# Seven products in place of eight for two K-tile pairs in ten of eleven feed-forward up strips

## The reference

```python
def swiglu(x, w_up, w_down):              # w_up (2048, 2*5632), w_down (5632, 2048)
    g, u = jnp.split(x @ w_up, 2, axis=-1)
    return (jax.nn.silu(g) * u) @ w_down

h = h + 0.5 * rms_norm(swiglu(rms_norm(h, ffn1_pre), ffn1_up, ffn1_down), ffn1_post)
h = h + rms_norm(hybrid_mixer(...), mix_post)
h = h + 0.5 * rms_norm(swiglu(rms_norm(h, ffn2_pre), ffn2_up, ffn2_down), ffn2_post)
```

## Time and profile before

| | us |
|---|---|
| median of 3 runs | 2435.23 |
| lowest and highest | 2434.61, 2436.49 |
| span of the profiled execution, first to last instruction | 2433.9 |
| PE busy in it | 2415.4 (99%) |
| DVE busy | 1289.5 (53%) |
| ACT busy | 1149.2 (47%) |

### The profile page before, as it was taken

The page is one execution under the profiler, slowest core; times in us unless marked ns, Lnnn a source line. Parts: engine busy times, 40 slices in busy tenths (PEclk is TensorE's granted clock), DMA queues, the critical chain, the costliest instruction groups (busy, mean ns, idle before and its releaser), DMA issues.

```text
span 2433.9 us, 32932 instructions
## 1 busy us (share of the span) xinstructions
PE 2415.4 (99%) x10823; PEld 1985.5 (82%) x10823; DVE 1289.5 (53%) x1395; ACT 1149.2 (47%) x1340; POOL 41.6 (2%) x48
## 2 busy tenths in 40 slices
PE   9999999999999999999999999999999999999998
PEld 7888888888887788887888888888888888888887
DVE  5455554544447555555545555555555555554444
ACT  6454544533435454454544444444554454544443
POOL 1000000000001000000000000000000000000000
PEclk9999999999999999999999999999999999999999
DMA  8566665766565555565656666655566665665664
GB/s 256 187 217 193 211 215 182 225 199 195 192 189 183 156 170 177 164 186 159 199 183 202 192 192 195 192 182 178 176 216 216 190 218 184 219 209 196 190 196 158
DMA packets 271357, 470.91 MB, mean 193 GB/s; under 512 B 21056, under 2 KB 65776, under 8 KB 270928
## 3 DMA queue, kind: packets, MB, share of 16 engines
q1 hardware_dynamic: 269648, 464.60, 61.2%
q0 software_dynamic: 1488, 5.68, 0.8%
q10 hardware_dynamic: 176, 0.07, 0.0%
HBM read 456.64 MB, written 2.10 MB: 188 GB/s over the span
## 4 chain that ended last, share of the span: by engine, by line
PE 94%; SPq 2%; DVE 2%; DMA 1%; ACT 1%; issue 1%; DVEq 0%; ACTq 0%; POOL 0%; POOLq 0%
PE acc L580 31%; PE acc L582 30%; PE acc L581 30%; SPq L424 2%; PE bank L601 1%; DMA w_raw<-in_ffn_up_dram 1%; DVE w_lo L1221 1%; ACT w_hi L923 0%; DMA w_raw<-in_ffn_down_dram 0%; PE bank L824 0%; PE bank L764 0%; PE bank L790 0%; DVE xT_lo L1232 0%; DVE hid_sb L1359 0%; PE bank L845 0%
## 5 line engine op out<-in xcount | busy, mean ns | idle before, releaser
L1221 DVE TENSOR_TENSOR w_lo<-w_raw,w_hi 128x1024 fp32r<-128x1024 f32 x856 | 1045.0, 1227 | 1062.1 <-ACT w_hi L923 1052.5
L923 ACT ACTIVATE w_hi<-w_raw 128x1024 fp32r<-128x1024 f32 x856 | 902.5, 1060 | 1192.7 <-PE acc L582 1040.3
L580 PE MATMUL acc<-w_hi,xT_hi 128*128 128x512 f32 x2464 | 968.8, 393 | 6.1 <-DVE xT_lo L1232 3.9
L582 PE MATMUL acc<-w_hi,xT_lo 128*128 128x512 f32 x2464 | 960.1, 390 | 0.0
L581 PE MATMUL acc<-w_lo,xT_hi 128*128 128x512 f32 x2464 | 959.6, 389 | 0.0
L580 PEld LDWEIGHTS acc<-w_hi,xT_hi 128*128 128x128 f32 x2464 | 463.0, 188 | 110.0 <-DVE w_lo L1221 7.6
L582 PEld LDWEIGHTS acc<-w_hi,xT_lo 128*128 128x128 f32 x2464 | 462.9, 188 | 97.0
L581 PEld LDWEIGHTS acc<-w_lo,xT_hi 128*128 128x128 f32 x2464 | 463.2, 188 | 95.2 <-issue 1.0
L580 PE MATMUL acc<-w_hi,act_hi 128*128 128x512 f32 x704 | 274.2, 389 | 1.5 <-DVE w_lo L1221 1.5
L581 PE MATMUL acc<-w_lo,act_hi 128*128 128x512 f32 x704 | 273.9, 389 | 0.0
L582 PE MATMUL acc<-w_hi,act_lo 128*128 128x512 f32 x704 | 273.9, 389 | 0.0
(11 more groups left out here) (144 smaller groups left out, 911.7 us busy)
## 6 DMA issues: line engine op xcount, KB each, us to landing
w_raw<-in_ffn_up_dram SPq DMA_DIRECT2D x352, 512.0 KB, 4.4
w_raw<-in_ffn_down_dram SPq DMA_DIRECT2D x176, 512.0 KB, 4.7
w_raw<-in_w_gate_dram SPq DMA_DIRECT2D x96, 512.0 KB, 4.1
w_raw<-in_w_in_dram SPq DMA_DIRECT2D x72, 512.0 KB, 3.7
w_raw<-in_w_in_dram SPq DMA_DIRECT2D x128, 256.0 KB, 3.0
w_raw<-in_w_ret_out_dram SPq DMA_DIRECT2D x32, 512.0 KB, 4.6
w_raw<-in_w_out_dram SPq DMA_DIRECT2D x32, 512.0 KB, 4.5
hid_T<-blocks SPq DMA_DIRECT2D x352, 32.0 KB, 1.8
```

Source lines behind the costliest of these rows:

```text
L580: pe.matmul(pair[m][:, :], xh, wh, start=(first and kk == 0), stop=False)
L582: mm = pe.matmul(pair[m][:, :], xl, wh, start=False, stop=(last and kk == KG - 1))
L923: act.activation(w_hi[:, s, :], w_raw[:, s, :], ACT.Copy).then_inc(w_rounded, 1)
L1221: dve.tensor_tensor(w_lo[:, s, :], w_raw[:, s, :], w_hi[:, s, :].bitcast(f32), ALU.subtract).then_inc(w_split, 1)
```

## The change

Strip 1 of each feed-forward block stays as it was (section `first{f}`). In the other ten, two of the eight K-tile pairs (K-tile pairs 6 and 7 of 0 to 7) are computed by Strassen's scheme over the 2x2 blocks token tile by K tile and K tile by gate/up. For such a pair PE makes 7 products of 3 passes (21 instructions) in place of 8 (24).

- DVE makes the four weight sums `t_raw` from the gate group and the up group of the pair (`sum13`, one operation of 1024 columns; `sum24`, two chained of 512). ACT rounds them, DVE takes their rests (two operations of 1024 columns each). In the up group only the second K tile is still split (512 columns).
- The four input sums `s_raw` are made once per block, during strip 1; PE transposes four scaled tiles for them, and waits for `s_split` ahead of the loop.
- PE's order in a strip: groups 0 to 3, pair by Strassen (groups 4 and 5), 6, 7, 8, 9, pair by Strassen (10 and 11), 12 to 15. Gate is complete at group 11.
- Products 1, 5, 6 and 7 go to four PSUM banks. DVE combines them: at step 11 and 12 the gate (`u2`, `u3`, `u4`, `u5`, `gate_sb`), at the end of the strip up (`hid_sb`, L1664 and L1666 of the changed kernel), then the product with the silu'd gate (L1671), then the block transposes. ACT's silu moves from step 7 to step 13.
- The turned activations go to `act_raw`, a place for each strip. Their split moves out of the up strips: the first two at steps 14 and 15 of the last up strip, the others at every second step of the first turn of down. PE's group `n` of down waits for the split of strip `n // 2`.
- `u2` to `u5` lie where `post_gain` is, so POOL loads `post_gain` only when the last up strip has been read. DVE waits for it ahead of the loop of down.

```diff
+QUADS = ((4, 5, 6), (10, 11, 7))
-                        sp.dma_start(hid_T[to * SQ:(to + 1) * SQ, q, :, :, :],
+                        sp.dma_start(act_raw[to * SQ:(to + 1) * SQ, ds(p, 1), q, :, :, :].rearrange("p a m k i -> p (a m) k i"),
                                      blocks[q * SQ:(q + 1) * SQ, to, :, :, :]).then_inc(hid_landed, 16)
...
+                with sp.Fori(0, NST) as i:
                     for n in range(2 * GD):
                         if n == 2 * SLOTS:
-                            with sp.If(i > 0):
-                                turn_hidden(f, before(i, NUP))
+                            turn_hidden(f, i)
+                        if n - SLOTS in QUAD_GATE:
+                            sp.wait_ge(t_summed, 3 * (quad(f, i, QUAD_GATE[n - SLOTS]) + 1))
+                            sp.sem_inc(slot_summed, 1)
...
+            rsqrt("pre2", rs_pre[:, 2, :])
+            wait_strip_read(pool, "up1", NST - 1, 1)
             pool.dma_start(post_gain[:, :], on_all(t["ffn2_post"][0], D)).then_inc(gain_landed, 16)
...
+            def seven_products(f, i, j):
...
+                pe.wait_ge(w_split, group(sec, i, ng) + 1 + SLOTS)
+                p1 = three(bank[0][:, :], *x(0), *w(ng, 0), first, last)
...
+                three(gate[0][:, :], *x(1), *w(ng, 1), False, last).then_inc(w_used, 1)
...
+                pe.wait_ge(w_split, group(sec, i, nu) + 1 + SLOTS)
+                three(upper[0][:, :], *s(3), *w(nu, 1), first, False).then_inc(w_used, 1)
+                pe.wait_ge(t_split, 2 * quad(f, i, j) + 1)
+                p7 = three(bank[3][:, :], *s(2), *tt(1), first, last)
+                p5 = three(bank[1][:, :], *s(0), *tt(0), first, last)
+                pe.wait_ge(t_split, 2 * quad(f, i, j) + 2)
+                p6 = three(bank[2][:, :], *s(1), *tt(2), first, last)
...
+                three(gate[1][:, :], *a22, *tt(3), False, last).then_inc(t_used, 1)
...
+                with dve.Fori(0, NST) as i:
                     for n in range(2 * GD):
+                        if n + SLOTS in QUAD_GATE:
+                            sum13(f, i, QUAD_GATE[n + SLOTS])
                         rest_group(sec, i, n)
+                        if n + SLOTS in QUAD_GATE:
+                            sum24(f, i, QUAD_GATE[n + SLOTS])
+                        if n in T_AT:
+                            j, pair = T_AT[n]
...
+                            dve.tensor_tensor(t_pair(t_lo, j, pair), t_pair(t_raw, j, pair),
+                                              t_pair(t_hi, j, pair).bitcast(f32), ALU.subtract).then_inc(t_split, 1)
...
+                    dve.wait_ge(silu_done, NST * f + i + 1)
+                    wait_strip_read(dve, sec, i, 1)
                     for m in range(MT):
+                        last = dve.scalar_tensor_tensor(hid_sb[:, m, :], hid_sb[:, m, :], rs_pre[:, 2 * f, m:m + 1],
+                                                        gate_sb[:, m, :], ALU.mult, ALU.mult)
+                    last.then_inc(combined, 1)
+                    wait_combined(dve, f, i, "hid")
+                    turn_blocks()
```

More of the change, by code:

```diff
@@ L91, in bank_uses, with strassen @@
     use("gains", 3)
+    def strassen(f):
+        use(f"s{f}", 2, 3)
+        for _ in range(NST):
+            use(f"p{f}", 0, 1, 2, 3)
     transposed("x0")
+    strassen(0)
     transposed("x1")
@@ L668, in tail, with three @@
                 tile_by_tile(product, range(total - SLOTS, total), {(1, SLOTS - 2): pieces})
-            def swiglu(f):
[L671 to L678, removed]
-                        head(product, i, lambda c, m: transpose_h(2, c, m))
-                    for n in range(SLOTS if f == 1 else 0, 2 * GD):
-                        product(n)
-                        if f == 0 and n in (0, 2, 4):
-                            with pe.If(i < 1):
-                                for half in range(2):
-                                    transpose_x(n // 2 + 1, half)
+            def three(dst, xh, xl, wh, wl, start, stop):
+                pe.matmul(dst, xh, wh, start=start, stop=False)
+                pe.matmul(dst, xh, wl, start=False, stop=False)
+                return pe.matmul(dst, xl, wh, start=False, stop=stop)
@@ L922, in round_it @@
                     act.wait_ge(w_used, group(sec, i, ahead) + 1)
-                    act.activation(w_hi[:, s, :], w_raw[:, s, :], ACT.Copy).then_inc(w_rounded, 1)
+                    cols = w_cols(sec, ahead)
+                    act.activation(w_hi[:, s, cols], w_raw[:, s, cols], ACT.Copy).then_inc(w_rounded, 1)
                 if sec == "kv" and ahead >= GD:
@@ L989, in hidden_hi @@
                 for m in range(MT):
-                    last = act.activation(act_tile(act_hi, p, m), hid_tile(m), ACT.Copy)
+                    last = act.activation(act_tile(act_hi, p, m), raw_tile(p, m), ACT.Copy)
                 last.then_inc(hid_rounded, 1)
@@ L1005, in output_strips @@
                     round_group(sec, i, n)
[L1006 to L1007 removed]
+                    if hook is not None:
+                        hook(n)
                 def tile0():
@@ L1028, in swiglu @@
             def swiglu(f):
+                sec = f"first{f}"
+                for n in range(2 * GD):
+                    round_group(sec, 0, n)
+                    if f == 0 and n in (0, 2):
+                        x_hi(n // 2 + 2)
+                    if n == (3 if f == 0 else 2):
+                        if f == 0:
+                            for c in range(CH):
+                                act.wait_ge(x_landed[c], 16)
+                        input_squares(2 * f)
+                    if n == GD - 1:
+                        wait_strip(act, sec, 0, n)
+                        act.wait_ge(rs_ready, MEAN[f"pre{2 * f}"] + 1)
+                        pair = pair_of(sec, 0)
+                        for m in range(MT):
+                            last = act.activation(gate_sb[:, m, :], acc[pair][m][:, :], ACT.Silu,
+                                                  scale=rs_pre[:, 2 * f, m:m + 1])
+                        last.then_inc(acc_read[pair], 1)
+                    if n == 13:
+                        act.wait_ge(s_summed, f + 1)
+                        act.activation(s_hi[:, :, :, :].rearrange("p a b n -> p (a b n)"),
+                                       s_raw[:, :, :, :].rearrange("p a b n -> p (a b n)"), ACT.Copy).then_inc(s_rounded, 1)
@@ new lines, in swiglu @@
+                        if n == 12:
+                            wait_read(dve, f"p{f}", 3, i)
+                            dve.scalar_tensor_tensor(gate_sb[:, 1, :], u3_sb[:, :], to_tile1[:, 0:1], gate[1][:, :],
+                                                     ALU.mult, ALU.add).then_inc(acc_read[pair_of(sec, 0)], 1)
+                            dve.tensor_tensor(u5_sb[:, :], u3_sb[:, :], bank[1][:, :], ALU.add).then_inc(read[1], 1)
+                        if n in (14, 15):
+                            with dve.If(i > NST - 2):
+                                hidden_lo(f, n - 14)
```

381 lines of the change are left out of this document (293 added, 88 removed).

## The result

The changed kernel takes 2513.03 us (median of 4 runs, 2511.55 to 2519.46), beside 2434.92 us of the kernel before on the same chip: ratio 1.0321, 95% interval 1.0309 to 1.0333. It is slower by 78 us, where 2536 us with a range of 2475 to 2580 was forecast. The profiled execution has a span of 2517.5 us, 83.6 over the 2433.9 of before, where the sum said +100.

The account below looks back on a forecast made before the run. PE, busy 99%, was taken as the bound, with group 8's load just in time behind SP's burst. Products -27.2, transposes +1, strip waits +118, first strips -1, start of down +9.6 gave +100 us: 2536 us, range 2475 to 2580.

Parts of the forecast that it names:

- The bound and the direction: PE bounds the kernel, with no slack for group 8 behind SP's DMA burst; slower by more than 0.2%, chance 0.92.
- Products and sums: On PE, 120 products less save 27.2 us; eight added transposes for the input sums cost 1 us.
- (a): PE reaches group 8 sooner in a changed strip, 93 products ahead of it in place of 96: 0.68 us.
- (b): DVE has four operations of 512 columns ahead of the transposes where it had two: +1.44 us a strip.
- (c): A register instruction for each of SP's 16 DMAs lengthens the burst ahead of group 8's load to 12.3 us, +2.3.
- Rival 1: Register instructions hide behind SP's DMAs, so the burst stays 10.0 us: +54, 2489 us; chance 0.17.
- The second pair and the clock: Groups 10 and 11: DVE's list makes PE wait 1.5 us more a strip, or a clock drop replaces that wait.
- the two first strips: First changed strip of each block: waits 1 us less in all, after an older, shorter strip end, despite 2 us for sums.
- The start of down: PE waits 2.2 us for strip 1's activation split, then 2.6 us behind DVE's wait for `post_gain`: 9.6 us over two blocks.
- How often the clock falls: By the skill's rule, every changed strip would show the low clock level after its wait; the sum holds with or without.
- Rival 3: Low clock lasts twice as many products, 3.2 us a strip, and the burst takes 13.7 us: +162, 2597 us; chance 0.10.
- Rival 2: SP's burst shrinks to 6.0 us ahead of group 8 because computed addresses are quick: faster, 2419 us; chance 0.06.

Follow-up runs that it names:

- The halves: Changed kernel with SP's 16 turning DMAs split, eight ahead of group 8's load and eight ahead of group 12's: 2428.13 us, ratio 0.9956.
- the POOL versions: Turning DMAs issued by POOL, not SP: changed kernel 2419.23 us, with three end waits also removed 2404.33 us; kernel before 2430.48 us.

## Why the prediction was right, and where it was off

- **The bound and the direction: right.** PE had no slack for group 8 behind SP's burst; what was added ahead of the burst came out as waits of PE, and a strip grew by more than its six products saved. The halves and the POOL versions show that all of it hangs on this one place.
- **Products and sums: right.** 112 instructions less, worth 26.6 us (-27.2 + 1 forecast).
- **(a), PE's earlier arrival, 0.68 us, and (b), two operations, 1.44 us: right.** The transposes end 1.5 us later in the strip, and two such operations in the kernel before cost 1.36 a strip at this place and nothing at another.
- **(c), the burst: the step that failed.** The text took 0.77 us a DMA, +2.3 a strip, "nearest to what the load rows do, where a gap is really there". Measured 0.664 (10.63 over 16), +0.6. The DMA's own length was forecast well: 0.529, where 0.528 was taken. The gap was not: 0.135 us (0.664 less 0.529), where 0.24 was taken from the loads. But a load has three register instructions ahead of it (`ALU_OP`, `FUSED_REGOPS`, `MOVE`) and a turning DMA one, so the load rows did not price what was added. Rival 1 came near in the number (10.0 us), but not in its mechanism: nothing hides behind a DMA of 0.59, the gap grew by 0.10 us and the DMA got 0.06 shorter. Why it got shorter was not tested. The wait for group 8 is therefore 2.8 us and not 4.4. By the Trainium skill's rule ("DMA: Bandwidth & Descriptors", section "Issuing engines are not separate DMA queues"), the issue time is usually small beside the DMA; in this case's trace it is 0.627 to 0.664 us for a DMA that lands after 1.8, and taking the 16 off SP brought 94 us (2513.03 to 2419.23), so for small DMAs ahead of a load on one engine the measurement decides against it.
- **The second pair and the clock: mechanism right, the term too small.** The forecast was 1.5 us a strip, either as waits in the second pair or as a fall of the clock in their place. Measured behind the wait for group 8: 2.0 us in the 6 strips without a fall, and 1.56 + 0.9 = 2.5 in the 12 with one, 2.3 on average. So a fall has the forecast size (1.6), but it takes away only 1.1 us of the second pair's waits, and on these averages costs 0.5 us net. The text also took the spread of the landings of groups 8 to 11 as the 5.1 us of one strip. In the strip shown ACT gets group 11 6.2 us behind group 8, after a gap of 2.62 ahead of group 10; in the strip at 339.9, which is 46.0 us long, that gap is 0.64 and the spread 4.2. With the halves these waits went with the one for group 8.
- **Sum.** From +100: (c) 1.6 too much in 18 strips, -29; the two first strips 3.2 and 4.8 for the sums where 10.8 was forecast, -3; second pair and clock +0.8 in 18, +15. That leaves +83, beside the measured 83.6. That the time came out within 23 us of 2536 owes something to luck, since two errors have opposite signs.
- **The start of down: sum right, parts not.** Forecast 2.2 and 2.6 in each block, 9.6 in all; `act_lo` measures 9.5, as 1.07 and 4.24 in the first block and 4.1 in the second, where the gains' wait was only 2.8. That the last burst stands ready behind it was not seen; moving the wait for the gains alone brought little that the measurement can tell.
- **How often the clock falls.** The Trainium skill ("TensorE: Matmul & The Clock Gate", section "HAM oscillation — how this bites in real kernels") tells of waits of about 3 to 5 us with a cold start behind every one, and by it the prediction expected the low level in every changed strip. Here the waits are 2.4 to 3.0 us, and it follows 12 of 18. Rival 3 did not come about: the low level lasts 7 or 8 products, once 13, and the whole span has a clock of 0.988.
- **Rival 2 (a faster burst): refuted in size.** The computed form takes 0.529 us here, not 0.372, and with its register instruction the pitch is 0.04 us longer than before. But what it rested on, that the sign hangs on SP ahead of group 8 alone, is so: with 5.2 us there the kernel is faster than before.

## What to carry to other kernels

Before arithmetic is taken off the engine that is always busy, look for the item that reaches it with no slack, and follow its chain back to the queue that issues it: here a burst of small DMAs ahead of a load turned a saving of 27 us into a loss of 78, and moving half of the burst, or its issue to an idle engine, made the kernel 10 to 18 us faster than before. The whole saving came once the waits at the ends of the blocks were gone too. An operation's price is its place: two operations on VectorE cost 30 us ahead of that burst and nothing in the middle of the strip. A gap between two instructions in a trace has to be read with what stands in it, before it is used as the price of one instruction. When a wait is removed and little is gained, read which item is late next in the same queue before calling the wait harmless.

## What the runs showed of the hardware

- On SP, 16 small DMAs (32x256) take 0.59 us each with 0.04 between them when they stand back to back, and 0.53 with 0.135 between them when one register instruction (0.046) stands ahead of each: 0.627 against 0.664 us a DMA. Loads take 0.37 each and stand 0.62 to 0.67 apart, with three register instructions ahead of each.
- POOL issues the same 16 DMAs in 8.66 us, 0.54 each, less than SP's 10.6, but each lands 3.7 us (median) after its issue, where from SP it takes 1.8.
- A wait of PE of 2.4 to 3.0 us was followed by half clock in 12 of 18 strips, for 7 or 8 products of 512 columns, once 13. What decides it stays open.
- Why the load of group 10 sometimes comes 2.6 us late behind the burst (strips of 46.0 and of 48.1 us) stays open too; in the strip shown it lands 7.5 us after its issue, groups 8 and 9 after 3.9 and 4.4.
